# A hybrid DiT layer on one core: where the residual's store stands in the DMA queue, the order of the last chunk of a first group, and who scales the output

## The chip, the cores and the metric

One NeuronCore of a Trainium2 chip runs the whole layer. The metric is device time in microseconds (us), the median of several executions. TensorE (PE) multiplies, VectorE (DVE), ScalarE (ACT) and GpSimd (POOL) work on elements, SyncE (SP) issues most DMAs. Each engine runs its own instructions in the order in which the program lists them and waits on semaphores, and so does SP: a DMA whose wait is not met holds back every DMA behind it.

## The reference

The input is 1024 latent tokens of width 1024 and 256 context tokens. The layer is a half-step SwiGLU FFN (width 2816), then two token mixers from one input projection (`w_in`, softmax attention and a gated linear attention), merged and projected, then a second half-step FFN and a final RMSNorm.

```python
def half_ffn(h, mod, i, g, w_up, w_down):
    shift, scale, gate = mod[..., 3 * i, :], mod[..., 3 * i + 1, :], mod[..., 3 * i + 2, :]
    return h + 0.5 * gate * swiglu(modulate(rms_norm(h, g), shift, scale), w_up, w_down)
...
        h = half_ffn(h, m_lat, 0, g_norm[l, 0], w_ffn_up[l, 0], w_ffn_down[l, 0])
        hc = half_ffn(hc, m_ctx, 0, g_norm[l, 0], w_ffn_up[l, 0], w_ffn_down[l, 0])
        n_lat = modulate(rms_norm(h, g_norm[l, 1]), m_lat[..., 3, :], m_lat[..., 4, :])
        p_lat = jnp.split(n_lat @ w_in[l], IN_SPLITS, axis=-1)
...
        h = h + m_lat[..., 5, :] * merge_branches(p_lat, attn_lat, gla_lat, g_gla[l], w_branch[l], b_gate[l], w_out[l])
        h = half_ffn(h, m_lat, 2, g_norm[l, 2], w_ffn_up[l, 1], w_ffn_down[l, 1])
    return rms_norm(h, g_final)
```

## The kernel before

**Layout.** Activations stand feature-major in SBUF: 8 tiles k of 128 features by tokens. Tokens come in chunks: 512, 512 and 256 (the context) in the first FFN (`ffn0`) and the input projection (`win`), 512 and 512 in the second FFN (`ffn1`). Every product is made of three float32r matmuls (`three`, L203 to L207), since both operands are split in a high and a low part: `nh`, `nl` (or `n1h`, `n1l`) for the normalized activations, `wh`, `wl` for the weights.

**Weight panels.** Weights arrive as panels of 128 x 1024 in `raw`, which has two slots. VectorE splits a panel into `wh` and `wl` (`split_panel`, L178), which also have two slots each. So the load of panel p waits until panel p-2 is split, and the split of panel p waits until TensorE is done with panel p-2 (`panel_used`). All loads go through SP's queue in program order.

**An FFN group.** `Ffn.pe` goes over 11 groups: four up panels (a, b, a, b; 8 tiles k for each chunk), SiLU on ScalarE, the product and its split on VectorE (`hidden`), and two down panels, whose results VectorE adds to `h`. In the first group of an FFN the normalization is still being made: panels 0 and 1 of a chunk are taken in pairs of tiles by `PAIR_STEPS` (`up_pair`), with a wait for tile k before each (`normed`), except for the last chunk. There TensorE waits once for the last tile, then takes panel 0 for all k, then panel 1. `win_pe` does the same for the first two panels of `w_in` (c == 2 is the last chunk).

**The norm between.** `Norm` squares on ScalarE, sums with matmuls (`sums`, L465), takes the root on ScalarE, the inverse on VectorE, and spreads it over partitions with matmuls into a PSUM bank (`spread`, L487). Then for each tile k: VectorE scales (L499), ScalarE rounds to the high part (L508), VectorE takes the low part (L516). For `ffn1`'s second chunk, `spread` is issued inside the pair steps of the first chunk (`norm2_rest_pe`, at step 11).

**The residual's store.** After `ffn0` the latent `h0` (4 MB) is saved to DRAM, since its SBUF space is needed. In `win_sp` this store stands behind the load of the first `w_in` panel and waits for the last add of `ffn0` (`wait_end`). ScalarE waits for it (`h_saved`) before it writes the first projection results over `h0`.

**The output.** In `ffn1`'s last group the down product goes chunk by chunk in 16 tiles q (six matmuls each). When chunk 0 is done (q up to 7), its four blocks of 128 tokens are turned by TensorE (`y_turn`) into two PSUM banks each, between the tiles of chunk 1; ScalarE squares and takes the root (`y_act`), VectorE takes the reciprocal and multiplies by it and by `g_final` (`y_scale`), SP stores 512 KB (`result_sp`). Then the four blocks of chunk 1. Blocks 2 and 3 use the banks of blocks 0 and 1.

Of the kernel before, what the change touches and what calls it, by code (L numbers as in the profile page):

```python
# [100 lines left out]
def build(nc, x, c, ctx_in, c_ctx, w_mod, b_mod, g_norm, w_ffn_up, w_ffn_down, w_in, g_q, g_k,  # L101
# [8 lines left out]
    def sem(name):  # L110
# [29 lines left out]
    y_ss, y_root, y_inv = at("y_ss", 181, [SEQ // P]), at("y_root", 181.125, [SEQ // P]), at("y_inv", 181.25, [SEQ // P])  # L140
    y_junk = at("y_junk", 174, [D])
    g_row = at("g_row", 201, [D])
    y_rows = at("y_rows", 72, [SEQ // P, D])
    h1 = at("h1", 40, [KT, SEQ])
    n1h, n1l = at("n1h", 0, [KT, SEQ], F32R), at("n1l", 72, [KT, SEQ], F32R)
# [28 lines left out]
    y_turned, y_squared, y_rooted, y_inverse, y_done = (  # L174
        sem(n) for n in ("y_turned", "y_squared", "y_rooted", "y_inverse", "y_done"))


    def split_panel(dve, p, n=1024):  # L178
# [17 lines left out]
    def wait_panel(pe, p):  # L196
# [2 lines left out]

    PAIR_STEPS = [(0, 0), (0, 1), (0, 2), (0, 3), (1, 0), (1, 1), (1, 2), (1, 3),  # L200
                  (0, 4), (1, 4), (0, 5), (1, 5), (0, 6), (1, 6), (0, 7), (1, 7)]

    def three(pe, o, hi_w, lo_w, hi_x, lo_x, first, last):  # L203

# [329 lines left out]
    class Ffn:  # L534
# [44 lines left out]
        def pe(self, pe, in_first, in_last):  # L579
# [22 lines left out]
            def up_pair(g, c):  # L602

                o = [up_bank(g, 0, c), up_bank(g, 1, c)]
                for n, (j, k) in enumerate(PAIR_STEPS):
                    self.norm.normed(pe, c, k)
                    mm = up_k(o[j], j, c, k)
                    if k == KT - 1:
                        mm.then_inc(self.up_done, 1)
                    in_first(c, n)  # L610

            def down(j, n, c, o):
# [7 lines left out]
            def body(g, first, last):  # L620
                if first:
                    wait_panel(pe, self.panel(g, 0))
                    wait_panel(pe, self.panel(g, 1))
                    for c in range(C - 1):
                        up_pair(g, c)
                    self.norm.normed(pe, C - 1, KT - 1)
                    for j in range(2):
                        up(g, j, C - 1)
                for j in range(2 if first else 0, 4):
                    wait_panel(pe, self.panel(g, j))  # L630
                    for c in range(C):
                        up(g, j, c)
                if last:
                    for q in range(8 * C):
                        c, j, n = q // 8, 4 + q % 8 // 4, q % 4
                        if n == 0 and c == 0:
                            wait_panel(pe, self.panel(g, j))
                        if q % 8 == 0:
                            pe.wait_ge(self.hid_done, g * (4 * C) + 2 * (C + c) + 2)
                        if q == 2:  # L640
                            pe.wait_ge(self.hid_done, (g + 1) * (4 * C))
                        pe.wait_ge(self.down_free, self.n_down + g * (8 * C) + max(0, q - 2))
                        mm = down(j, n, c, ps[self.TAIL_BANKS[q % 3]][:, 0:self.chunks[c][1]])
                        mm.then_inc(panel_used if n == 3 and c == C - 1 else self.down_done, 1)
                        in_last(q)
                    return
                for j in range(4, 6):
                    wait_panel(pe, self.panel(g, j))
                    for n in range(4):
                        for c, (t0, w) in enumerate(self.chunks):  # L650
                            i = ((j - 4) * 4 + n) * C + c
                            if j == 4 and n == 0:
                                pe.wait_ge(self.hid_done, g * (4 * C) + 2 * (C + c) + 2)
                            pe.wait_ge(self.down_free, g * (8 * C) + (i + 1))
                            mm = down(j, n, c, ps[self.down_banks[i % self.n_down]][:, 0:w])
                            mm.then_inc(self.down_done if not (n == 3 and c == C - 1) else panel_used, 1)
# [108 lines left out]
    def y_turn(pe, i):  # L765

        ffn1.wait_residual(pe, 7 if i < 4 else 15)
        if i in (2, 3):
            pe.wait_ge(y_done, i - 1)
        if i in (6, 7):  # L770
            pe.wait_ge(y_done, i - 3)
# [11 lines left out]
    def y_scale(dve, i):  # L783
        dve.wait_ge(y_rooted, i + 1)
        nc.vector.reciprocal(y_inv[:, i:i + 1], y_root[:, i:i + 1]).then_inc(y_inverse, 1)
        if i == 0:
            dve.wait_ge(g_row_loaded, 16)
        dve.wait_ge(y_inverse, i + 1)
        nc.vector.scalar_tensor_tensor(y_rows[:, i, :], y_psum(i), y_inv[:, i:i + 1], g_row[:, :], ALU.mult, ALU.mult)\
            .then_inc(y_done, 1)  # L790

    def result_pe(pe, q):

        if q >= 9 and q % 2 == 1:
            y_turn(pe, (q - 9) // 2)
        if q == 15:
            for i in range(4, 8):
                y_turn(pe, i)

    def result_act(act):  # L800
        for i in range(SEQ // P):
            y_act(act, i)

    def result_dve(dve):
        for q in range(16):
            ffn1.last_residual(dve, q)
            if q in (12, 14):
                y_scale(dve, (q - 12) // 2)
        for i in range(2, SEQ // P):
            y_scale(dve, i)  # L810

    def result_sp(sp):
        for i in range(SEQ // P):
            sp.wait_ge(y_done, i + 1)
# [82 lines left out]
    def win_sp(sp, panel0, ffn0, norm):  # L897
        w = w_in[0].rearrange("(k p) n -> p k n", p=P)
        for i, (col, width, _, _) in enumerate(win):
            p = panel0 + i  # L900
            load_panel(sp, pn(p), raw[:, p % 2, 0:KT * width].rearrange("p (k n) -> p k n", k=KT),
                       w[:, :, col:col + width])
            if i == 0:
                ffn0.wait_end(sp)
                sp.dma_start(h_dram, h0[:, :, 0:SEQ]).then_inc(h_saved, 16)

# [49 lines left out]
    def win_pe(pe, panel0, norm):  # L956
# [14 lines left out]
        wait_panel(pe, pn(panel0))  # L971
        ffn0.wait_residual(pe, 22)
        for c in range(3):
            if c == 2:
                norm.normed(pe, c, KT - 1)
                for j in range(2):
                    for k in range(KT):
                        mm = unit_k(2 * c + j, k)
                    done(2 * c + j, mm)
                continue  # L980
            if c == 1:
                ffn0.wait_residual(pe, 23)
            for n, (j, k) in enumerate(PAIR_STEPS):
                if (c, j, k) == (0, 1, 0):
                    wait_panel(pe, pn(panel0 + 1))
                norm.normed(pe, c, k)
# [1016 lines left out]
    @block.gpsimd  # L2003
    def _(pool):
        att_pool(pool)

    @block.vector
    def _(dve):
# [61 lines left out]
```

## Time and profile before

| | us |
|---|---|
| time, median of 3 runs | 3090.2 (3086.2 to 3090.93) |
| the profiled execution's own time | 3087.16 |
| its span, first to last instruction | 3085.1 |
| busy: PE, DVE, ACT, POOL | 2882.0, 1499.4, 552.3, 59.5 |
| mean granted TensorE clock, share of full speed | 0.957 |

A row of a timeline is: start, duration, engine, line, operation, output<-inputs, shape, count, and in brackets the time that the engine sat idle before it with what ended the idle time. Matmuls overlap: with 512 columns each shows 0.39 us and the next one starts earlier than it ends.

### The profile page before, as it was taken

What the parts mean: (1) busy time and instruction counts of PE and PEld (TensorE: products, weight loads), DVE (VectorE), ACT (ScalarE), POOL (GpSimd) and SP (SyncE); (2) the same over time, 40 slices, a digit from 0 to 9 for tenths busy, and PEclk for the clock granted to TensorE, in tenths of its full rate; (3) what the DMA queues carried; (4) which work ended last, traced back from release to release, by engine and by line L of the source; (5) the groups of instructions that cost most, each with busy time, mean ns of one, the idle gap of its engine ahead of it and who ended that gap; (6) DMA issues with size and microseconds to landing.
All of it is one profiled execution on the core that took longest, in us unless ns stands there. A gap on an engine that the chain in (4) does not pass through costs nothing. (4 is left out here: it accounts for less than half of the span.)

```text
span 3085.1 us, 35899 instructions
## 1 busy us (share of the span) xinstructions
PE 2882.0 (93%) x14410; PEld 2298.4 (75%) x14410; DVE 1499.4 (49%) x2403; ACT 552.3 (18%) x1035; POOL 59.5 (2%) x100
## 2 busy tenths in 40 slices
PE   8999999999999799999956859998998999999998
PEld 2588888888888587888245637776877888888887
DVE  5544444444444611111596378886644444444444
ACT  3200000000000311111422247774011000000001
POOL 0000000000000000000000001121000000000000
PEclk9999999999999899999876569999999999999999
DMA  8511111111111211233400100002430111111111
GB/s 289 161 35 41 41 34 41 34 41 34 41 40 36 76 37 48 82 99 103 140 1 1 41 0 1 1 1 69 142 97 27 48 49 48 48 48 41 47 55 69
DMA packets 190653, 176.15 MB, mean 57 GB/s; under 512 B 5805, under 2 KB 147290, under 8 KB 190554
## 3 DMA queue, kind: packets, MB, share of 16 engines
q1 hardware_dynamic: 184794, 164.29, 17.2%
q10 hardware_dynamic: 5760, 10.49, 0.9%
q8 instruction: 69, 1.13, 0.2%
q14 instruction: 30, 0.25, 0.0%
HBM read 155.89 MB, written 18.87 MB: 57 GB/s over the span
## 5 line engine op out<-in xcount | busy, mean ns | idle before, releaser
L205 PE MATMUL psum<-nh,wh 128*128 128x512 f32 (+2 forms) x1688 | 613.6, 364 | 16.0 <-DVE wl L185 15.4
L206 PE MATMUL psum<-nl,wh 128*128 128x512 f32 (+2 forms) x1688 | 613.1, 363 | 0.0
L207 PE MATMUL psum<-nh,wl 128*128 128x512 f32 (+2 forms) x1688 | 612.7, 363 | 0.0
L183 DVE CAST wh<-raw 128x1024 fp32r<-128x1024 f32 x175 | 120.2, 687 | 727.3 <-PE psum L207 699.7
L205 PEld LDWEIGHTS psum<-nh,wh 128*128 128x128 f32 (+1 forms) x1688 | 317.3, 188 | 68.1 <-DVE wl L185 15.5
L206 PEld LDWEIGHTS psum<-nl,wh 128*128 128x128 f32 (+1 forms) x1688 | 317.3, 188 | 50.7
L207 PEld LDWEIGHTS psum<-nh,wl 128*128 128x128 f32 (+1 forms) x1688 | 317.0, 188 | 51.1
L716 DVE SCALAR_TENSOR_TENSOR h<-psum,gates,h 128x512 f32<-128x512 f32 (+1 forms) x400 | 270.9, 695 | 143.6 <-PE psum L207 140.6
L205 PE MATMUL psum<-hidh,wh 128*128 128x512 f32 (+1 forms) x880 | 328.2, 373 | 8.0 <-DVE hidl L700 7.6
L684 ACT ACTIVATE silu_a<-psum 128x512 f32<-128x512 f32 (+1 forms) x110 | 61.2, 556 | 1495.2 <-PE psum L207 1495.2
L206 PE MATMUL psum<-hidl,wh 128*128 128x512 f32 (+1 forms) x880 | 324.9, 369 | 0.0
L207 PE MATMUL psum<-hidh,wl 128*128 128x512 f32 (+1 forms) x880 | 324.0, 368 | 0.0
L205 PE MATMUL psum<-n1h,wh 128*128 128x512 f32 x704 | 275.2, 391 | 8.5 <-DVE n1l L516 8.5
L207 PE MATMUL psum<-n1h,wl 128*128 128x512 f32 x704 | 274.7, 390 | 0.0
L206 PE MATMUL psum<-n1l,wh 128*128 128x512 f32 x704 | 274.7, 390 | 0.0
L695 DVE TENSOR_TENSOR prod<-silu_a,psum 128x512 f32<-128x512 f32 (+1 forms) x110 | 69.9, 635 | 344.9 <-PE psum L207 343.7
L185 DVE TENSOR_TENSOR wl<-raw,wh 128x1024 fp32r<-128x1024 f32 x175 | 213.7, 1221 | 6.0
L205 PEld LDWEIGHTS psum<-hidh,wh 128*128 128x128 f32 x880 | 165.9, 188 | 43.6 <-issue 13.7
L207 PEld LDWEIGHTS psum<-hidh,wl 128*128 128x128 f32 x880 | 165.6, 188 | 28.5
L206 PEld LDWEIGHTS psum<-hidl,wh 128*128 128x128 f32 x880 | 166.0, 189 | 26.7
L205 PEld LDWEIGHTS psum<-n1h,wh 128*128 128x128 f32 x704 | 132.7, 188 | 36.7 <-DVE n1l L516 8.9
L207 PEld LDWEIGHTS psum<-n1h,wl 128*128 128x128 f32 x704 | 132.6, 188 | 27.6
(239 smaller groups left out, 3382.9 us busy)
## 6 DMA issues: line engine op xcount, KB each, us to landing
raw<-in_w_ffn_up_dram SPq DMA_DIRECT2D x88, 512.0 KB, 3.8
mod_raw<-in_w_mod_dram SPq DMA_DIRECT2D x24, 1024.0 KB, 5.1
raw<-in_w_ffn_down_dram SPq DMA_DIRECT2D x44, 512.0 KB, 3.8
raw<-in_w_in_dram SPq DMA_DIRECT2D x34, 512.0 KB, 3.8
mod_raw_late<-in_w_mod_dram SPq DMA_DIRECT2D x12, 1024.0 KB, 5.1
gates_saved<-staged ACTq DMA_DIRECT2D x40, 256.0 KB, 2.0
merge_gate<-gates_saved SPq DMA_DIRECT2D x8, 1024.0 KB, 5.1
x_rows<-in_x_dram SPq DMA_DIRECT2D x8, 512.0 KB, 7.4
```

What stands on the lines that cost most here:

```text
L183: nc.vector.tensor_copy(wh[:, par, 0:n], raw[:, par, 0:n]).then_inc(panel_split, 1)
L185: nc.vector.tensor_tensor(wl[:, par, 0:n], raw[:, par, 0:n], wh[:, par, 0:n].bitcast(F32), ALU.subtract).then_inc(panel_split, 1)
L205: pe.matmul(o, hi_w, hi_x, start=first, stop=False)
L206: pe.matmul(o, hi_w, lo_x, start=False, stop=False)
L207: return pe.matmul(o, lo_w, hi_x, start=False, stop=last)
L684: nc.scalar.activation(silu_a[:, c, 0:w], ps[c][:, 0:w], ACT.Silu).then_inc(self.a_free, 1)
L695: nc.vector.tensor_tensor(prod[:, c % 2, 0:w], silu_a[:, c, 0:w], ps[3 + c][:, 0:w], ALU.mult).then_inc(self.b_free, 1)
L716: nc.vector.scalar_tensor_tensor(hk, down, gates[:, self.gate_i, k, s:s + 1], hk, ALU.mult, ALU.add).then_inc(self.down_free, 1)
```

## The change

Four edits. The store of `h0` stands behind the third panel load of `win_sp` and no longer behind the first. The last chunk of `ffn0`'s, `ffn1`'s and `win`'s first two panels is taken tile by tile in a new order, `LAST_PAIR_STEPS`, with a wait for each tile. `spread` of `ffn1`'s second chunk is issued at pair step 8 and no longer at step 11. The output of chunk 0 is scaled by ScalarE from PSUM into a new buffer (`y_copy`), and multiplied by `g_final` on GpSimd (`y_gain`); the turns of these blocks come one tile q earlier, and they wait for the copy out of PSUM only. VectorE keeps their reciprocals, and the whole of chunk 1.

```diff
+    LAST_PAIR_STEPS = [(0, 0), (0, 1), (0, 2), (0, 3), (1, 0), (0, 4), (1, 1), (0, 5),
+                       (1, 2), (0, 6), (1, 3), (0, 7), (1, 4), (1, 5), (1, 6), (1, 7)]
...
-                for n, (j, k) in enumerate(PAIR_STEPS):
+                for n, (j, k) in enumerate(PAIR_STEPS if c < C - 1 else LAST_PAIR_STEPS):
                     self.norm.normed(pe, c, k)
                     mm = up_k(o[j], j, c, k)
                     if k == KT - 1:
-                        mm.then_inc(self.up_done, 1)
+                        mm.then_inc(self.up_done if c < C - 1 else panel_used, 1)
...
-                    for c in range(C - 1):
+                    for c in range(C):
                         up_pair(g, c)
-                    self.norm.normed(pe, C - 1, KT - 1)
-                    for j in range(2):
-                        up(g, j, C - 1)
...
         if i in (2, 3):
-            pe.wait_ge(y_done, i - 1)
+            pe.wait_ge(y_copied, i - 1)
...
+    def y_copy(act, i):
+        act.wait_ge(y_inverse, i + 1)
+        nc.scalar.activation(y_scaled[:, i, :], y_psum(i), ACT.Copy, scale=y_inv[:, i:i + 1]).then_inc(y_copied, 1)
+
+    def y_gain(pool, i):
         if i == 0:
+            pool.wait_ge(g_row_loaded, 16)
+        pool.wait_ge(y_copied, i + 1)
+        nc.gpsimd.tensor_tensor(y_rows[:, i, :], y_scaled[:, i, :], g_row[:, :], ALU.mult).then_inc(y_gained, 1)
...
     def result_pe(pe, q):
 
-        if q >= 9 and q % 2 == 1:
-            y_turn(pe, (q - 9) // 2)
+        if q >= 8 and q % 2 == 0:
+            y_turn(pe, (q - 8) // 2)
...
             load_panel(sp, pn(p), raw[:, p % 2, 0:KT * width].rearrange("p (k n) -> p k n", k=KT),
                        w[:, :, col:col + width])
-            if i == 0:
+            if i == 2:
                 ffn0.wait_end(sp)
                 sp.dma_start(h_dram, h0[:, :, 0:SEQ]).then_inc(h_saved, 16)
...
-            for n, (j, k) in enumerate(PAIR_STEPS):
+            for n, (j, k) in enumerate(PAIR_STEPS if c < 2 else LAST_PAIR_STEPS):
...
-        if (c, n) == (0, 11):
+        if (c, n) == (0, 8):
             norm2.spread(pe, 1)
```

SP's queue at the end of `ffn0` before the change: the last panels of the FFN, one panel of `w_in`, the store, and the other panels.

```order
L194 DMA raw<-in_w_ffn_up_dram 128x8x128 x4
L194 DMA raw<-in_w_ffn_down_dram 128x2x512 x2
L194 DMA raw<-in_w_in_dram 128x8x128
L905 DMA h_saved<-h_49 1024x1x1024
L194 DMA raw<-in_w_in_dram 128x8x128 x7
```

The same place in the changed kernel:

```order
L195 DMA raw<-in_w_ffn_up_dram 128x8x128 x4
L195 DMA raw<-in_w_ffn_down_dram 128x2x512 x2
L195 DMA raw<-in_w_in_dram 128x8x128 x3
L929 DMA h_saved<-h_49 1024x1x1024
L195 DMA raw<-in_w_in_dram 128x8x128 x5
```

The loads of panels 1 and 2 of `w_in` now stand ahead of the store; panel 3 is the first behind it.

ScalarE's last instructions before the change, for the first three output blocks (a square with its sum, and a root, for each):

```order
L778 ACTIVATE y_junk,y_ss<-psum 128x1024
L780 ACT_TABLE_LOAD
L780 ACTIVATE y_root<-y_ss,cols_b 128x1
L778 ACTIVATE y_junk,y_ss<-psum 128x1024
L780 ACTIVATE y_root<-y_ss,cols_b 128x1
L778 ACTIVATE y_junk,y_ss<-psum 128x1024
```

And in the changed kernel:

```order
L779 ACTIVATE y_junk,y_ss<-psum 128x1024
L781 ACT_TABLE_LOAD
L781 ACTIVATE y_root<-y_ss,cols_b 128x1
L790 ACTIVATE y_scaled<-psum,y_inv 128x1024
L779 ACTIVATE y_junk,y_ss<-psum 128x1024
L781 ACTIVATE y_root<-y_ss,cols_b 128x1
L790 ACTIVATE y_scaled<-psum,y_inv 128x1024
```

A copy of 128x1024 has been put in after each of the first four roots; it needs VectorE's reciprocal, so the next square stands behind that too.

VectorE at the same place before the change (L749 adds a down tile to `h`, L785 is the reciprocal, L789 the product with `g_row`):

```order
L749 SCALAR_TENSOR_TENSOR h_89<-psum,gates,h_89 128x512 x13
L785 RECIPROCAL y_inv<-y_root 128x1
L789 SCALAR_TENSOR_TENSOR y_rows<-psum,y_inv,g_row 128x1024
L749 SCALAR_TENSOR_TENSOR h_89<-psum,gates,h_89 128x512 x2
L785 RECIPROCAL y_inv<-y_root 128x1
L789 SCALAR_TENSOR_TENSOR y_rows<-psum,y_inv,g_row 128x1024
L749 SCALAR_TENSOR_TENSOR h_89<-psum,gates,h_89 128x512
```

And in the changed kernel:

```order
L750 SCALAR_TENSOR_TENSOR h_90<-psum,gates,h_90 128x512 x11
L786 RECIPROCAL y_inv<-y_root 128x1
L750 SCALAR_TENSOR_TENSOR h_90<-psum,gates,h_90 128x512 x2
L786 RECIPROCAL y_inv<-y_root 128x1
L750 SCALAR_TENSOR_TENSOR h_90<-psum,gates,h_90 128x512 x2
L786 RECIPROCAL y_inv<-y_root 128x1
L750 SCALAR_TENSOR_TENSOR h_90<-psum,gates,h_90 128x512
```

Between the adds only reciprocals are left; the four products of chunk 0 are gone from VectorE.

## Rows read from the trace of the kernel before

**Rows 1.** The page, part 1: busy us, share of the span, instructions

```profile
PE 2882.0 (93%) x14410; PEld 2298.4 (75%) x14410; DVE 1499.4 (49%) x2403; ACT 552.3 (18%) x1035; POOL 59.5 (2%) x100
```

**Rows 2.** Waits of TensorE, whole span: us in total, times, longest

```profile
PE psum L205 <- DVE wl L185: 22.3, 3, 15.4
...
PE psum L205 <- DVE n1l L516: 8.5, 1, 8.5
```

**Rows 3.** Timeline of SP's queue, 984 to 1100 us

```profile
987.99 0.37 SPq L194 DMA_DIRECT2D raw<-in_w_in_dram  x1
1042.22 0.63 SPq L905 DMA_DIRECT2D h_saved<-h  x1
1042.89 47.75 SPq L194 DMA_DIRECT2D raw<-in_w_in_dram  x5
```

**Rows 4.** Timeline of VectorE, 1000 to 1100 us, the panels' splits

```profile
1001.56 1.23 DVE L185 TENSOR_TENSOR wl<-raw,wh 128x1024 fp32r<-128x1024 f32 x1
...
1038.46 1.23 DVE L185 TENSOR_TENSOR wl<-raw,wh 128x1024 fp32r<-128x1024 f32 x1
...
1057.96 0.69 DVE L183 CAST wh<-raw 128x1024 fp32r<-128x1024 f32 x1 [15.77 <-DMA raw<-in_w_in_dram]
1058.69 1.23 DVE L185 TENSOR_TENSOR wl<-raw,wh 128x1024 fp32r<-128x1024 f32 x1
...
1085.41 0.69 DVE L183 CAST wh<-raw 128x1024 fp32r<-128x1024 f32 x1 [3.31 <-PE psum L207]
```

**Rows 5.** Timeline of TensorE, 1020 to 1120 us

```profile
1044.16 0.43 PE L465 MATMUL psum<-sq,cst 128*32 128x64 f32 x16
1059.97 0.79 PE L205 MATMUL psum<-nh,wh 128*128 128x512 f32 x1 [15.38 <-DVE wl L185]
...
1088.02 0.40 PE L205 MATMUL psum<-nh,wh 128*128 128x512 f32 x1
```

**Rows 6.** DMA issues: count, KB each, median us to landing

```profile
h_saved<-h SPq DMA_DIRECT2D x1, 4096.0 KB, 13.3
...
out_dram<-y_rows SPq DMA_DIRECT2D x8, 512.0 KB, 2.7
```

**Rows 7.** Windows: length, busy of each engine, PEclk, DMA share, GB/s

```profile
1060.00:1064.00 4.00, 4.00 (x10) 3.13 (x11) 4.00 (x7) 1.64 (x3) 0.00 (x0) 0.50 0.50 131
...
200.00:1040.00 840.00, 839.56 (x4495) 715.97 (x4494) 364.43 (x548) 48.91 (x89) 0.00 (x0) 1.00 0.12 36
```

**Rows 8.** Timeline of VectorE, 2300 to 2385 us

```profile
2337.22 0.75 DVE L516 SCALAR_TENSOR_TENSOR n1l<-scaled_t,modv,n1h 128x512 fp32r<-128x512 f32 x1
...
2345.15 1.62 DVE L516 SCALAR_TENSOR_TENSOR n1l<-scaled_t,modv,n1h 128x512 fp32r<-128x512 f32 x2
...
2349.18 0.69 DVE L700 TENSOR_TENSOR hidl<-prod,hidh 128x512 fp32r<-128x512 f32 x1
```

**Rows 9.** Timeline of TensorE, 2332 to 2362 us

```profile
2334.59 1.05 PE L487 MATMUL psum<-inv_t,cst 128*128 128x128 f32 x8
...
2337.99 0.39 PE L207 MATMUL psum<-n1h,wl 128*128 128x512 f32 x1
2346.83 0.80 PE L205 MATMUL psum<-n1h,wh 128*128 128x512 f32 x1 [8.45 <-DVE n1l L516]
...
2359.54 0.39 PE L207 MATMUL psum<-n1h,wl 128*128 128x512 f32 x1
2359.76 0.39 PE L205 MATMUL psum<-n1h,wh 128*128 128x512 f32 x1
```

**Rows 10.** Timeline of TensorE in the tail: the first turn

```profile
3059.18 1.03 PE L773 MATMUL psum<-cst,h 128*128 128x128 f32 x8
```

**Rows 11.** Timeline of VectorE in the tail: the last product

```profile
3080.73 1.28 DVE L789 SCALAR_TENSOR_TENSOR y_rows<-psum,y_inv,g_row 128x1024 f32<-128x1024 f32 x1
```

**Rows 12.** Groups of ScalarE by shape: the squares (busy us, mean ns, idle)

```profile
L778 ACT ACTIVATE y_junk<-psum 128x1024 f32<-128x1024 f32 x8 | 8.1, 1016 | 33.1 <-PE psum L773 33.1
```

**Rows 13.** Groups of GpSimd: a product of two tensors

```profile
L1770 POOL TENSOR_TENSOR att_t<-att_t,att_rb 64x256 f32<-64x256 f32 x32 | 23.2, 725 | 2069.8 <-DVE att_t L1744 2069.8
```

More of the change, by code:

```diff
@@ L142, in build @@
     g_row = at("g_row", 201, [D])
+    y_scaled = at("y_scaled", 0, [4, D])
     y_rows = at("y_rows", 72, [SEQ // P, D])
@@ L173, in build @@
     g_row_loaded = sem("g_row_loaded")
-    y_turned, y_squared, y_rooted, y_inverse, y_done = (
-        sem(n) for n in ("y_turned", "y_squared", "y_rooted", "y_inverse", "y_done"))
+    y_turned, y_squared, y_rooted, y_inverse, y_copied, y_gained, y_done = (
+        sem(n) for n in ("y_turned", "y_squared", "y_rooted", "y_inverse", "y_copied", "y_gained", "y_done"))
     def split_panel(dve, p, n=1024):
@@ L768, in y_turn @@
         if i in (2, 3):
-            pe.wait_ge(y_done, i - 1)
+            pe.wait_ge(y_copied, i - 1)
         if i in (6, 7):
-            pe.wait_ge(y_done, i - 3)
+            pe.wait_ge(y_copied, i - 3)
         for k in range(KT):
@@ L781, in y_act, with y_reciprocal, y_scale @@
             .then_inc(y_rooted, 1)
-    def y_scale(dve, i):
+    def y_reciprocal(dve, i):
         dve.wait_ge(y_rooted, i + 1)
         nc.vector.reciprocal(y_inv[:, i:i + 1], y_root[:, i:i + 1]).then_inc(y_inverse, 1)
+    def y_copy(act, i):
+        act.wait_ge(y_inverse, i + 1)
+        nc.scalar.activation(y_scaled[:, i, :], y_psum(i), ACT.Copy, scale=y_inv[:, i:i + 1]).then_inc(y_copied, 1)
+    def y_gain(pool, i):
         if i == 0:
+            pool.wait_ge(g_row_loaded, 16)
+        pool.wait_ge(y_copied, i + 1)
+        nc.gpsimd.tensor_tensor(y_rows[:, i, :], y_scaled[:, i, :], g_row[:, :], ALU.mult).then_inc(y_gained, 1)
+    def y_scale(dve, i):
+        if i == 4:
             dve.wait_ge(g_row_loaded, 16)
+        y_reciprocal(dve, i)
         dve.wait_ge(y_inverse, i + 1)
@@ L802, in result_act @@
             y_act(act, i)
+            if i < 4:
+                y_copy(act, i)
     def result_dve(dve):
@@ L806, in result_dve, with result_pool @@
             ffn1.last_residual(dve, q)
-            if q in (12, 14):
-                y_scale(dve, (q - 12) // 2)
-        for i in range(2, SEQ // P):
+            if q >= 10 and q % 2 == 0:
+                y_reciprocal(dve, (q - 10) // 2)
+        y_reciprocal(dve, 3)
+        for i in range(4, SEQ // P):
             y_scale(dve, i)
+    def result_pool(pool):
+        for i in range(4):
+            y_gain(pool, i)
     def result_sp(sp):
         for i in range(SEQ // P):
-            sp.wait_ge(y_done, i + 1)
+            if i < 4:
+                sp.wait_ge(y_gained, i + 1)
+            else:
+                sp.wait_ge(y_done, i - 3)
             sp.dma_start(out[0, i * P:(i + 1) * P, :], y_rows[:, i, :]).then_inc(out_stored[i % 2], 16)
@@ L973, in win_pe @@
         for c in range(3):
[L974 to L980, printed above, removed]
             if c == 1:
                 ffn0.wait_residual(pe, 23)
-            for n, (j, k) in enumerate(PAIR_STEPS):
+            for n, (j, k) in enumerate(PAIR_STEPS if c < 2 else LAST_PAIR_STEPS):
                 if (c, j, k) == (0, 1, 0):
@@ L2005, in _ @@
         att_pool(pool)
+        result_pool(pool)
     @block.vector
```

## The prediction

> **What bounds the kernel now.** I read the busy shares first: TensorE is busy for 2882 of 3085 us [rows 1], so most of the change's places lie on its path, and what it can win there is TensorE's idle time and the clock that it loses by idling. The waits of TensorE [rows 2] give the idle time. Two single waits matter: 15.4 us for the low half of a weight panel (`wl`), and 8.5 us for the last tile of a normalization (`n1l`). Then I read the timelines around both.
>
> The first wait is the change from `ffn0` to `win`. SP loads panel 0 of `w_in` at 987.99 and then stands in the wait of the store until 1042.22; panel 1's load goes out behind the store at 1042.89 [rows 3]. The store takes 13.3 us to land [rows 6] and the panel lands behind it: VectorE has sat idle for 15.77 us when its cast starts at 1057.96, and TensorE goes on at 1059.97, 15.38 us late [rows 4, 5]. The second is the first group of `ffn1`: TensorE is through with chunk 0 at 2338.2 and waits until tile 7 of chunk 1 is ready, 2346.8 [rows 8, 9].
>
> **The store behind panel 2's load.** Panel 1's load then waits for one thing only, the split of the panel two before it, which ends at 1001.56 + 1.23 = 1002.8 [rows 4]; at 15 us or less it has landed long before it is wanted. Panel 2's load waits for the split of panel 0 and goes out at 1038.46 + 1.23 = 1039.7, still ahead of the last add of `ffn0`, so the store leaves at 1042.2 as before. VectorE starts panel 1's split where its idle time began, 1057.96 - 15.77 = 1042.2, and ends at 1044.1; TensorE is done with its 16 small sums at about 1044.55 [rows 5] and goes on at once. That is the whole 15.4 us. What is late next? Panel 3's load: it waits for panel 1's split (1044.1) and lands behind the store at about 1059; it is wanted by its split at about 1070, 11 us of cover. ScalarE's wait for the store: that lands at 1042.2 + 13.3 = 1055.5, and ScalarE is busy with the norm's high parts for another 10 us. VectorE's tiles: its whole chain moves forward by 15.8 us with TensorE, so none is late that was not.
>
> **The clock.** After the pause the granted clock was 0.50 for the 4 us from 1060 to 1064 [rows 7], the lower level of 1.2 GHz; half of these 4 us is lost work, 2.0 us. With no pause ahead of it I take that back too.
>
> **The last chunk tile by tile, in `win`.** TensorE waited only a few tenths there, which I leave in the noise. But the new order has a price. Panel 2 can be split only when panel 0 is used up, and a split takes 0.69 + 0.04 + 1.23 = 1.96 us. Before, the cast began at 1085.41, when eight tiles of panel 1 were left, and TensorE needed panel 2 at 1088.02: 2.61 us, enough. 24 matmuls of 256 columns are 2.9 us, so one is 0.12. Now four tiles are left when panel 0 is done, 12 matmuls or 1.44 us less: 2.61 - 1.44 = 1.17 us for 1.96 us of work, a new wait of 0.8 us. `win` together: 15.4 + 2.0 - 0.8 = **16.6 us**.
>
> **`ffn0`.** The same order, the same 256 columns, and no wait for tiles to remove, since that norm is finished long before. So only the price: **-0.8 us**.
>
> **`ffn1`.** Two edits. `spread` comes three steps earlier; a step is three matmuls at 0.227 us (2359.54 to 2359.76 is one pitch), so 2.05 us: it moves from 2334.59 to 2332.5, and VectorE's chain on chunk 1 with it. The low parts end at 2337.97 (tile 0) and from there one in 1.32 us (2337.22 to 2345.15 is six tiles), the last at 2346.77 [rows 8]. Shifted: 2335.9, 2337.2, 2338.6, 2339.9, 2341.2, 2342.5, 2343.8, 2344.7. TensorE begins chunk 1 at 2338.2 and takes one step per 0.68 us; by the new order it wants tile 3 at 2340.3, tile 4 at 2341.6, tile 5 at 2343.0, tile 6 at 2344.4, tile 7 at 2345.7. Every one is there 0.4 us or more ahead. So chunk 1 ends at 2338.2 + 48 x 0.227 = 2349.1, where it ended at 2359.76 [rows 9]. Here too panel 2 is next. VectorE first finishes `hidden` of chunk 0, at 2349.18 + 0.69 - 2.05 = 2347.8 (ScalarE's SiLU stands behind the high parts, which moved by the same), then splits: 2349.75. TensorE waits 0.6 us. 2359.76 - 2349.75 = **10.0 us**, of which 8.5 are the wait and the rest mostly the slow matmuls after it. Without the earlier `spread`, tiles come 2.05 us later and TensorE would lose 1.7 us to them.
>
> **The tail.** The first turn was at 3059.18 [rows 10]; it moves up by one tile (1.36 us) to 3057.8. From there seven tiles q and four turns of 0.8 us follow, none of which waits if ScalarE's copies come in time. A copy of 128x1024 out of PSUM is priced by the square of the same shape, 1.02 us [rows 12], and the chain square, root, reciprocal, copy gives copies done at about 3063.5, 3067.2, 3070.8 and 3073.5; the turns that need the first two come at 3065.0 and 3068.7. The last add of chunk 1 ends at about 3071.8. ScalarE reaches block 4's root at 3075.0, and VectorE's four products at 1.39 each end at 3080.6, where the last one ended at 3082.0 [rows 11]: 1.4 us. GpSimd's product is not in the trace at this size. Its product of 64x256 takes 0.725 us [rows 13]; four times the columns is at most 2.9 us, and VectorE's own product, 1.28, is the bound below. I take 2.9: the four end at 3066.4, 3070.1, 3073.7 and 3076.6. Then five stores of 512 KB leave from 3076.6 on. That stores land faster than one per 1.39 us the trace doesn't show; at that pace the last lands at 3076.7 + 4 x 1.39 + 2.7 = 3085.0 against 3084.8 before [rows 6]. So the tail is worth -0.2 to 1.4 us; I take the middle, **0.6**. In a sentence of its own: the Trainium skill ("GPSIMD Engine Reference", section 3.1) advises against elementwise products on GpSimd, at 4497 ns for 2048 columns against 2293 on VectorE; half of that, 2.25 us as an estimate, would let the last product end 0.65 us sooner than mine does, so the rule's price does no harm where the work is off the path.
>
> **Sum.** 16.6 - 0.8 + 10.0 + 0.6 = 26.4 us. The profiled execution took 3087.16 us, so it would be 3060.8. That execution is 3.0 us below the median of the three runs; from the median it is 3063.8. I put the forecast between, at 3062. A change under 0.2% (6 us) is about what a measurement can't tell from none.
>
> **The rivals.**
> 1. *One of the two big waits comes back in part (3070, chance 0.08).* In `ffn1` the tiles lead TensorE by only 0.4 us, and a wait that then starts would be repaid tile by tile; in `win` panel 3 may be late behind the store. Against it: a lead of 0.4 us costs at most what the chain is late in all (1.7 us by the sum above), and 11 us of cover. Half of the 10 us and 3 of `win` lost give 3070.
> 2. *The tail loses (3073, 0.03).* SP stores in order, so blocks 4 to 7 stand behind GpSimd's last product. If that product took twice my bound, 5.8 us, the four would end from 3069.3 to 3086.7, and five stores at 1.39 us would land at 3095.0, 10.2 us after the present end: 3062 + 0.6 + 10.2 = 3073. Against it: four times the row of 0.725 us is all that the width can cost if time goes with columns. Up to 2.9 us the tail loses nothing to speak of; from about 3.7 us on each product waits for the one before, and each further 1 us costs 4.
> 3. *The store's move doesn't do it (3077, 0.04).* If panel 1 were held by something else, or ScalarE's wait for the store stood on the path, 15 us stay. The queue's rows speak against it: the issue came 0.04 us after the store's.
> 4. *Slower (3100, 0.02).* The pauses are the only rests of TensorE in its dense stages; without them the chip might grant less clock. TensorE is dense for some 1880 us, so the gain is gone at 26.4 / 1880 = 1.4% less clock, and 3100 needs 1.9%. Against it: 840 us at 99.9% busy were granted 1.00 throughout, and the only low clock nearby came after a pause [rows 7].
>
> **How the numbers follow.** My forecast has 0.81. The runs before spread over 4.7 us, which the range must hold: from 3086.2 - 26.4 - 2 for tail and new waits, 3057.5, to rival 1's edge, 3069. That leaves out rivals 2, 3 and 4, and part of 1. All cases but rival 4 are over 0.2% faster; a small chance goes to no change, 0.02.
>
> **What would show it.** Right: no idle time of VectorE for `in_w_in`; TensorE's waits for `wl` at three places of 0.6 to 0.9 us; the wait for `n1l` gone, with no clock of 0.50 near either place; GpSimd's product between 2.2 and 2.9 us; last product on VectorE about 1.4 us nearer to the last turn's start. Wrong: a wait for `raw` on panel 3, waits for `n1l` or `nl` in pieces, stores queued behind GpSimd, or another granted clock in the attention stages, where it stood between 0.5 and 1 and where a shift of 16 us may fall out either way.

## The result, and the profile after

The changed kernel takes 3060.28 us in the median of 4 runs (3057.38 to 3064.43); the kernel before took 3088.38 on the same chip (3086.2 to 3090.93). The ratio is 0.991, with a 95% interval of 0.9893 to 0.9927: 28.1 us less. The forecast was 3062, the range 3057.5 to 3069. The profiled execution took 3064.43 us, the slowest of its four; its span is 3062.6 us and its mean clock 0.959, where the one of before had 3085.1 and 0.957.

The busy times of the page of the changed kernel, as in [rows 1]:

```profile
PE 2882.0 (94%) x14410; PEld 2300.6 (75%) x14410; DVE 1494.6 (49%) x2399; ACT 556.8 (18%) x1039; POOL 69.0 (2%) x104
```

TensorE's busy time and count are the same to the last digit, but that is chance, since it moved in every part. Windows over `win`'s first panels (stretch B below), before and after, with the columns of [rows 7]:

```profile
1042.20:1093.70 51.50, 36.12 (x190) 30.14 (x190) 27.32 (x45) 14.72 (x28) 0.00 (x0) 0.83 0.41 133
...
1044.40:1079.20 34.80, 34.12 (x190) 28.85 (x189) 27.12 (x45) 14.70 (x27) 0.00 (x0) 1.00 0.51 173
```

The same 190 matmuls take 2.00 us less of busy time, since none of them runs at the granted clock of 0.50 any more, and from stretch D on it is 2.27 less (731.05 for 733.32). Ahead of the store it is 2.16 more (1031.10 for 1028.94) and in stretch C 2.15 more (1085.75 for 1083.60), where the instructions are the same but for the order of one chunk; the last section takes up C. TensorE's waits for `wl`, as in [rows 2], and no row for `n1l` any more:

```profile
PE psum L209 <- DVE wl L186: 9.0, 5, 6.3
```

The longest, 6.3 us, was one of the three of before too (22.3 in all less 15.4 leaves 6.9 for two). SP's queue, as in [rows 3]:

```profile
990.17 52.10 SPq L195 DMA_DIRECT2D raw<-in_w_in_dram  x3
1044.40 0.63 SPq L929 DMA_DIRECT2D h_saved<-h  x1
1046.26 43.69 SPq L195 DMA_DIRECT2D raw<-in_w_in_dram  x4
```

Three loads now go ahead of the store, and panel 3's goes out 1.9 us behind it, when panel 1 has been split. The timeline of VectorE from 1044 us on, as in [rows 4]:

```profile
1044.29 0.68 DVE L184 CAST wh<-raw 128x1024 fp32r<-128x1024 f32 x1
...
1071.43 0.70 DVE L184 CAST wh<-raw 128x1024 fp32r<-128x1024 f32 x1 [3.00 <-PE psum L211]
1072.16 1.23 DVE L186 TENSOR_TENSOR wl<-raw,wh 128x1024 fp32r<-128x1024 f32 x1
```

The 15.77 us in which VectorE waited for the panel are gone. The cast at 1071.43 is panel 2's, and now it waits for TensorE to use up panel 0. The timeline of TensorE in the same stretch, as in [rows 5]:

```profile
1046.34 0.43 PE L469 MATMUL psum<-sq,cst 128*32 128x64 f32 x16
...
1073.44 0.50 PE L209 MATMUL psum<-nh,wh 128*128 128x512 f32 x1 [0.68 <-DVE wl L186]
```

The same timeline at the same step of `ffn0`, and in `ffn1` as in [rows 9]:

```profile
146.02 0.50 PE L209 MATMUL psum<-nh,wh 128*128 128x512 f32 x1 [0.68 <-DVE wl L186]
...
2337.96 0.50 PE L209 MATMUL psum<-n1h,wh 128*128 128x512 f32 x1 [0.51 <-DVE wl L186]
```

These are the three small waits that the forecast put at 0.8, 0.8 and 0.6 us. The windows of the two places, as in [rows 7]: the clock is at its higher level of 2.4 GHz (1.00) throughout, and TensorE busy for 28.76 of 29.40 us and 12.49 of 13.00 us.

```profile
1044.00:1073.40 29.40, 28.76 (x167) 24.39 (x165) 25.70 (x45) 15.10 (x27) 0.00 (x0) 1.00 0.49 174
2325.00:2338.00 13.00, 12.49 (x56) 10.01 (x55) 11.54 (x18) 6.66 (x9) 0.00 (x0) 1.00 0.00 0
```

**The tail.** Before the change TensorE's turns waited for VectorE's products, which held the PSUM banks: two of the three places on its timeline (the third waited 0.52 us):

```profile
3067.61 1.06 PE L773 MATMUL psum<-cst,h 128*128 128x128 f32 x8 [1.02 <-DVE y_rows L789]
...
3072.40 3.68 PE L773 MATMUL psum<-cst,h 128*128 128x128 f32 x32 [0.97 <-DVE y_rows L789]
```

In the changed kernel no turn waits for a product; the one wait left is for the last add of chunk 1:

```profile
3050.27 3.71 PE L774 MATMUL psum<-cst,h 128*128 128x128 f32 x32 [0.84 <-DVE h L750]
```

On the timeline of ScalarE, the third copy out of PSUM:

```profile
3048.07 1.12 ACT L790 ACTIVATE y_scaled<-psum,y_inv 128x1024 f32<-128x1024 f32 x1 [1.20 <-DVE y_inv L786]
```

On the timeline of GpSimd, the last product:

```profile
3051.94 2.37 POOL L796 TENSOR_TENSOR y_rows<-y_scaled,g_row 128x1024 f32<-128x1024 f32 x1 [0.32 <-ACT y_scaled L790]
```

On the timeline of VectorE, its first product and its last, as in [rows 11]:

```profile
3053.50 1.28 DVE L803 SCALAR_TENSOR_TENSOR y_rows<-psum,y_inv,g_row 128x1024 f32<-128x1024 f32 x1
...
3057.66 1.28 DVE L803 SCALAR_TENSOR_TENSOR y_rows<-psum,y_inv,g_row 128x1024 f32<-128x1024 f32 x1
```

And the DMA issues, as in [rows 6]:

```profile
h_saved<-h SPq DMA_DIRECT2D x1, 4096.0 KB, 13.0
...
out_dram<-y_rows SPq DMA_DIRECT2D x8, 512.0 KB, 2.9
```

GpSimd is through with its fourth product (block 3) at 3054.31, VectorE with its first (block 4) at 3054.78, 0.47 us later, and with its last at 3058.94.

**Where the time came from.** To add the parts up, I cut both traces at the same instructions. The cuts are: VectorE's second product of `ffn0`'s first group (A begins), the issue of the store (B), ScalarE's first gate of `win`'s panel 2 (C), VectorE's last add of the merge (D), ScalarE's SiLU of `ffn1`'s panel 2 (E), the end of VectorE's last product (F, up to the end of the span). B's beginning in the changed kernel is the store above. VectorE's rows for the beginnings of A and D:

```profile
139.64 0.69 DVE L696 TENSOR_TENSOR prod<-silu_a,psum 128x512 f32<-128x512 f32 x1 [9.00 <-PE psum L211]
...
2313.65 0.75 DVE L1947 SCALAR_TENSOR_TENSOR h<-psum,gates,h 128x512 f32<-128x512 f32 x1 [4.62 <-PE psum L211]
```

ScalarE's rows for those of C and E:

```profile
1079.22 0.60 ACT L1035 ACTIVATE gk_f<-psum 128x512 f32<-128x512 f32 x1 [6.03 <-PE psum L211]
...
2343.73 0.60 ACT L685 ACTIVATE silu_a<-psum 128x512 f32<-128x512 f32 x1 [8.37 <-PE psum L211]
```

So B, for one, is 1079.22 - 1044.40 = 34.82 us. The same differences for every kernel of this study, each from its one profiled execution:

| kernel | A `ffn0` | B `win` | C | D `ffn1` | E | F stores |
|---|---|---|---|---|---|---|
| before | 903.79 | 51.47 | 1231.77 | 39.94 | 716.61 | 3.09 |
| after | 904.76 | 34.82 | 1234.43 | 30.08 | 715.21 | 3.66 |
| c0 after again | 904.73 | 34.83 | 1233.98 | 30.08 | 715.20 | 3.67 |
| c1 store only | 903.81 | 35.60 | 1233.50 | 39.96 | 716.58 | 3.18 |
| c2 steps only | 904.76 | 52.34 | 1234.22 | 30.07 | 716.47 | 3.16 |
| c3 tail only | 903.66 | 50.95 | 1231.99 | 39.91 | 715.10 | 3.68 |
| c4 row order | 903.82 | 33.89 | 1232.14 | 30.10 | 715.09 | 3.72 |
| c5 spread at 11 | 904.76 | 34.84 | 1233.63 | 32.16 | 715.23 | 3.70 |
| c6 gain twice | 904.61 | 34.83 | 1234.12 | 30.08 | 715.08 | 10.09 |
| c7 store at 1 | 904.73 | 34.82 | 1234.21 | 30.08 | 715.10 | 3.71 |
| c9 all three | 903.67 | 33.87 | 1234.64 | 29.28 | 715.35 | 3.63 |
| c10 store twice | 904.62 | 34.84 | 1233.62 | 30.08 | 715.20 | 3.67 |
| c11 split first | 904.73 | 34.84 | 1228.57 | 29.28 | 715.20 | 3.70 |
| c12 row and split | 903.79 | 33.88 | 1235.67 | 29.28 | 715.21 | 3.69 |

From before to after: A -0.97, B +16.65, D +9.86, E +1.40, F -0.57. That is 26.4 us. The spans differ by 22.5, since C, whose instructions are the same in both, took 2.66 us more, and the stretch ahead of A 1.21 more. A, B, D, E and F repeat within 0.16 us where nothing in them was changed, but for one thing: the pause in B is not the same from run to run. TensorE's wait after it, in c3 and in c2:

```profile
1060.91 0.80 PE L206 MATMUL psum<-nh,wh 128*128 128x512 f32 x1 [14.89 <-DVE wl L186]
...
1063.13 0.80 PE L209 MATMUL psum<-nh,wh 128*128 128x512 f32 x1 [16.01 <-DVE wl L186]
```

With 15.38 before that is a spread of 1.1 us in three executions, so a gain in B against the one trace of before is known to about half a us, and no better. C does not repeat, and is taken up at the end.

A wait costs more than its number in brackets. A matmul of 512 columns shows 0.39 us, but the next one starts 0.227 us after it, and the first one behind a wait takes 0.34 us to the next start: 0.16 + 0.11 = 0.27 us on top of each bracket.

### The profile page after: what moved, and what is told of

Its sections match the earlier page's. It is cut to its first block and busy times, and to the rows that moved or that the text cites. A ratio compares the mean times of both kernels' runs of the same rounds, so it can differ in the third digit from the quotient of the medians.

```text
span 3062.6 us, 35904 instructions
## 1 busy us (share of the span) xinstructions
PE 2882.0 (94%) x14410; PEld 2300.6 (75%) x14410; DVE 1494.6 (49%) x2399; ACT 556.8 (18%) x1039; POOL 69.0 (2%) x104
```

## The experiments

**c0, c1, c2, c3: the change again, and its three parts alone.** c0 is the changed kernel as it is. c1 is the kernel before with one edit:

```diff
             load_panel(sp, ...)
-            if i == 0:
+            if i == 2:
                 ffn0.wait_end(sp)
```

c2 is the changed kernel with the store back at `i == 0` and the tail of before, so that the new order of steps and the earlier `spread` remain. c3 is the kernel before with the tail of the changed one.

> The changed kernel once more, as the measure for the others. If the split of the gain by places is right (16.8 us in win, 10.0 in ffn1, 0.8 lost in ffn0, 0.8 won in the tail), 26 to 27 us less than before, and the same four numbers in its trace. If the 28 us of the medians are the change's own, and not the spread of runs, the extra 1 to 2 us must turn up at one of these places.

> Only the store's place changed. My theory: the 15.4 us wait goes and so do 2.0 us of half clock after it; but TensorE now reaches the last chunk of win while its tiles are still made, and since it waits once for the last of them it loses about 1.4 us there: 16 us less than before. Rival: the wait was also held by the store's drain through ScalarE, then 5 us or less are won. Rival: the clock falls in win anyway, then 14 us.

> Only the order of the last chunks and the earlier spread. My theory: 10.0 us won in ffn1, 0.8 lost in ffn0, 0.6 lost in win (the store's wait stays there and hides nothing of it): 8.6 us less than before. Rival: in ffn1 the new order only spreads the wait over the tiles, then 3 us or less are won.

> Only the output of chunk 0 on ScalarE and GpSimd. My theory: VectorE's last product ends 1.4 us nearer to the end of ffn1's last group, and the last store lands 0.6 us later after it, so 0.8 us less than before, too little for the medians to tell; the trace of the tail must show it. Rival: ScalarE's longer chain makes the tail 1 us longer or more.

Medians, with the kernel before at 3091.18 us on this chip:

| kernel | us | ratio, 95% | less than before |
|---|---|---|---|
| c0 | 3062.71 | 0.9909 (0.9894 to 0.9924) | 28.5 |
| c1 | 3074.24 | 0.9948 (0.9934 to 0.9961) | 16.9 |
| c2 | 3081.66 | 0.997 (0.996 to 0.9981) | 9.5 |
| c3 | 3089.58 | 0.9998 (0.9988 to 1.0007) | 1.6 |

The parts add up to 28.0 us against 28.5 for the whole, so the medians don't show them to lean on each other; but their intervals are 6 to 9 us wide, and could not. The traces are finer, and show that inside `win` they do. TensorE's one wait in that part of c1:

```profile
1067.66 0.39 PE L205 MATMUL psum<-nh,wh 128*128 128x256 f32 x1 [1.44 <-DVE nl L516]
```

Before, no wait for `nl` stood there: the norm went on while TensorE stood still for the panel. With the pause gone the norm's last tile is late, and c1 wins 15.87 us in B, not the 17.4 of pause and clock. Taking the last chunk with a wait for each tile takes that wait away; with its 0.27 it is worth 1.71 us. In c2, where the pause is still there, the new order wins nothing: B is 0.87 us longer than before. That isn't all its price, since the pause alone was 0.63 us longer in this run; what the trace shows of the order is a new wait for `wl` of 0.68 us. VectorE's cast of panel 1 in c2:

```profile
1061.12 0.69 DVE L184 CAST wh<-raw 128x1024 fp32r<-128x1024 f32 x1 [16.42 <-DMA raw<-in_w_in_dram]
```

c3's tail wins 1.51 us in E and gives back 0.59 in F: 0.9, and its median can't tell that from nothing.

**c4: the last chunk of `ffn0` and `win` row by row.** The waits for each tile stay, but all eight tiles go through panel 0 first, then through panel 1, so eight tiles are left when panel 2 may be split, as before.

```diff
+    ROW_STEPS = [(j, k) for j in range(2) for k in range(KT)]
...
-                for n, (j, k) in enumerate(PAIR_STEPS if c < C - 1 else LAST_PAIR_STEPS):
+                for n, (j, k) in enumerate(PAIR_STEPS if c < C - 1 else ROW_STEPS if self.f == 0 else LAST_PAIR_STEPS):
...
-            for n, (j, k) in enumerate(PAIR_STEPS if c < 2 else LAST_PAIR_STEPS):
+            for n, (j, k) in enumerate(PAIR_STEPS if c < 2 else ROW_STEPS):
```

> The changed kernel, but in ffn0 and win the last chunk is taken panel by panel again, with a wait for each tile (panel 0 for all k, then panel 1). My theory: the two new waits of 0.7 us for wl go, since panel 0 is used up eight tiles before the end, and no wait for tiles comes in their place, since in win VectorE makes one tile in 0.79 us from 1063.0 on and TensorE wants tile 7 at about 1069.4: 1.4 us less than the changed kernel. Rival: the tiles are late in win, and 1 us of wait for nl takes the place of the 0.7.

Measured with c5, c6 and c7 beside 3089.47 for before: 3061.64 us, ratio 0.9912 (0.9897 to 0.9927). In the trace TensorE waits for nothing in B; A is 0.94 and B 0.93 us shorter than in the changed kernel. A is back at what it was before the change. So the price of the new order is the split of panel 2, and the place of that split sets it: a wait of 0.68 us and the 0.27 behind it, 0.95. Against c1, whose order is the same but for the one wait for all tiles, B is 1.71 us shorter: 1.44 + 0.27. B is now 17.58 us under before; pause and clock were put at 17.4, and the pause is uncertain by half a us.

**c5: `spread` at step 11 as before.** What the earlier `spread` is worth, with tiles in the new order:

```diff
-        if (c, n) == (0, 8):
+        if (c, n) == (0, 11):
```

> The changed kernel with the spread of ffn1's second chunk back at step 11. My theory: the tiles come 2.05 us later, TensorE waits for n1l in pieces of 0.3 to 0.7 us, hidden of chunk 0 and the split of panel 2 come 2.05 us later too: ffn1 loses 2.0 us against the changed kernel. Rival: the tiles lead TensorE by enough and nothing changes.

3063.62 us, ratio 0.9917 (0.9903 to 0.993). D is 2.08 us longer. Timeline of TensorE in `ffn1`'s first group:

```profile
2324.33 0.40 PE L211 MATMUL psum<-n1h,wl 128*128 128x512 f32 x1
2325.00 0.50 PE L209 MATMUL psum<-n1h,wh 128*128 128x512 f32 x1 [0.27 <-DVE n1l L520]
2325.34 0.39 PE L210 MATMUL psum<-n1l,wh 128*128 128x512 f32 x1
...
2326.32 0.50 PE L209 MATMUL psum<-n1h,wh 128*128 128x512 f32 x1 [0.36 <-DVE n1l L520]
...
2327.64 0.50 PE L209 MATMUL psum<-n1h,wh 128*128 128x512 f32 x1 [0.36 <-DVE n1l L520]
...
2337.46 0.50 PE L209 MATMUL psum<-n1h,wh 128*128 128x512 f32 x1 [0.67 <-DVE wl L186]
```

The wait for `n1l` comes back in pieces, each the gap between VectorE's pace (a tile in 1.32 us: 2326.32 to 2327.64) and TensorE's. D's growth is the whole 2.05 us by which `spread` is later, though those three pieces and the 0.16 more for `wl` are 1.15 us. Most of the rest stands in the starts: from 2324.33 to 2325.34 two matmuls take 1.01 us where 0.45 is their pace, so the first piece costs 0.56 and not 0.27. The three together cost 1.82 by their starts, with the 0.16 that is 1.98 of the 2.08.

**c6: GpSimd's product twice.** A second product into a buffer that nobody reads, ahead of each of the four, makes GpSimd's work in the tail twice as long:

```diff
+        nc.gpsimd.tensor_tensor(y_twice[:, i, :], y_scaled[:, i, :], g_row[:, :], ALU.mult)
         nc.gpsimd.tensor_tensor(y_rows[:, i, :], y_scaled[:, i, :], g_row[:, :], ALU.mult).then_inc(y_gained, 1)
```

> The changed kernel with each of GpSimd's four products done twice (once into a spare buffer), 4.8 us for a block. My theory: the products chain and the fourth ends at about 19.2 us after the first began, 3061.3 in the changed kernel's time; SP then issues five stores in a row. At the pace of one store in 1.39 us the end comes 7 to 8 us later than in the changed kernel; if stores land faster when they queue, one in 1.0 us, 5.5 to 6 us later. Rival: the DMA queue takes five stores at once, then 2.5 us.

3067.99 us, ratio 0.993 (0.9917 to 0.9944). That is 4.4 us more than c7, whose times are those of the changed kernel (3063.58, below), and F is 6.4 us longer; the 2 us between lie within the spread of the runs. The timeline of GpSimd, its last product:

```profile
3057.55 2.34 POOL L798 TENSOR_TENSOR y_rows<-y_scaled,g_row 128x1024 f32<-128x1024 f32 x1
```

And the window from 3060 to 3065, when only stores were left:

```profile
3060.00:3065.00 5.00, 0.00 (x0) 0.00 (x0) 0.00 (x0) 0.00 (x0) 0.00 (x0) 0.50 0.87 347
```

The product ends at 3059.89, VectorE was done at 3058.11, and all five stores left leave from 3059.91 on, the last at 3062.8, so SP issues them faster than they land. The span ends at 3068.2, 8.3 us later, where one store alone takes 3.09 (F of before): (8.3 - 3.09) / 4 = **1.30 us** for each further store of 512 KB. That is the number that the trace of before did not have. It also gives the end of the changed kernel. There, the store of block 3 leaves at 3054.31 and four follow: 3054.31 + 4 x 1.30 + 3.09 = 3062.60, and the span is 3062.6. By VectorE's last product alone it would be 3058.94 + 3.09 = 3062.03; the 0.57 us between are F's growth. In c6 GpSimd's fourth product ends 1.78 us after VectorE's last, in the changed kernel 4.63 us ahead of it: 6.41 us, and F grew by 6.43. So GpSimd's last product and the queue behind it set the end, and each us that this product took longer would be a us of the whole.

**c7: the store behind panel 1's load, not panel 2's.**

```diff
-            if i == 2:
+            if i == 1:
```

> The changed kernel with the store behind the load of panel 1 of w_in, not panel 2. My theory: panel 2's load then lands behind the store at about 1060, and its split isn't due before 1071, so nothing changes: within 1 us of the changed kernel. Rival: the store delays the next panels past their splits, then a new wait of VectorE for raw and 2 us or more lost.

3063.58 us, ratio 0.9913 (0.9898 to 0.9928); each stretch from A to F is that of c0 within 0.25 us. SP's queue:

```profile
990.67 15.20 SPq L195 DMA_DIRECT2D raw<-in_w_in_dram  x2
1044.88 0.63 SPq L929 DMA_DIRECT2D h_saved<-h  x1
1045.56 44.87 SPq L195 DMA_DIRECT2D raw<-in_w_in_dram  x5
```

Panel 2's load now stands behind the store, lands 14.3 us after its issue, at 1059.9, and still comes in time for its cast at 1071.92. All of the 15.4 us hangs on panel 1's load alone.

**c9, c11, c12: what is left of the small waits.** c11 splits panel 2 of `ffn1` ahead of `hidden` of chunk 0:

```diff
+                if first and self.f == 1:
+                    split_panel(dve, self.panel(g, 2))
+                    hidden(g, 0, range(C))
-                if first:
+                elif first:
                     hidden(g, 0, range(C - 1))
                     split_panel(dve, self.panel(g, 2))
```

c12 is c11 with c4's order. c9 is both, and VectorE's last product and its store in two halves of 512 columns:

```diff
-        nc.vector.scalar_tensor_tensor(y_rows[:, i, :], ...)
+        for cols in ([slice(0, 512), slice(512, D)] if i == 7 else [slice(0, D)]):
+            nc.vector.scalar_tensor_tensor(y_rows[:, i, cols], ...)
```

> The changed kernel, only with VectorE's split of panel 2 ahead of hidden of chunk 0 in ffn1's first group. My theory: the wait of 0.5 us for wl in ffn1 goes, and nothing else moves: 0.5 us, to be seen in the trace alone. Rival: hidden of chunk 0 comes 2 us later and holds up the up panels' banks.

> The changed kernel with three edits: in ffn0 and win the last chunk panel by panel with a wait for each tile; in ffn1's first group VectorE splits panel 2 ahead of hidden of chunk 0; VectorE's last product in two halves of 512 columns, each with a store of its own. My theory: 1.9 us from the first (0.9 in each), 0.5 us from the second, and 0.3 to 0.6 us from the third, since the last store is half as large but the queue is near its pace: 2.8 us less than the changed kernel, 29 to 31 less than before. Rival for the third: two stores cost the second's issue and nothing is won.

> The changed kernel with the last chunk panel by panel in ffn0 and win, and panel 2's split first in ffn1, without the halved last product. By the traces of the single edits: 0.9 us in ffn0, 0.9 in win, 0.8 in ffn1, 2.7 us less than the changed kernel in these segments and no wait of TensorE for wl in any of them; of the medians that is a third of their spread.

c11: 3060.56 us, ratio 0.9911 (0.9894 to 0.9927), and c9: 3060.01, 0.9905 (0.9889 to 0.9922), beside 3090.24 for before; c12: 3058.98, 0.9905 (0.9888 to 0.9921), beside 3087.81. In c11 D is 0.80 us shorter and the wait for `wl` is gone; c12 has A, B and D each as in the single edits, together 2.7 us under the changed kernel. The medians differ by less than their runs spread, so that rests on the traces. The halves won nothing. The timeline of VectorE in c9, its last product:

```profile
3053.76 1.41 DVE L809 SCALAR_TENSOR_TENSOR y_rows<-psum,y_inv,g_row 128x512 f32<-128x512 f32 x2
```

SP's queue, the second half's issue:

```profile
3055.19 0.75 SPq L848 DMA_DIRECT2D out_dram<-y_rows  x1
```

And the DMA issues, the half stores:

```profile
out_dram<-y_rows SPq DMA_DIRECT2D x2, 256.0 KB, 3.1
```

Two halves take 1.41 us for the 1.28 of the whole and the second issue alone 0.75. Above all the end does not hang on the last product, but on the queue from GpSimd's fourth product on (c6), and the queue has the same bytes to store: that product ends at 3050.41, and 3050.41 + 4 x 1.30 + 3.09 = 3058.70, where the span is 3058.8.

**c10: the store twice.** A second store of `h0` into a tensor of its own, right behind the first, and both are waited for. What does a store twice as long do to panel 3, whose cover was put at 11 us?

```diff
+                sp.dma_start(h_dram2, h0[:, :, 0:SEQ]).then_inc(h_saved, 16)
```

> The changed kernel with the 4 MB residual stored twice in a row (to two places; ScalarE and the later load wait for both). It measures the cover. The second store lands at about 25 us after the first's issue, panel 3 of w_in some 4 us behind it, 30 us after the issue. If my 11 us of cover is all there is, the split of panel 3 is late and time is lost, 1 to 2 us. If the cover is larger, since TensorE doesn't want panel 3 before it is through with panel 2, nothing changes, and only VectorE waits for raw.

3061.67 us, ratio 0.9914 (0.9897 to 0.9931), and A to F as in c0 within 0.4 us. SP's queue, the second store:

```profile
1043.57 2.38 SPq L931 DMA_DIRECT2D h_saved<-h  x1
```

The timeline of VectorE, the casts of panels 2 and 3:

```profile
1069.93 0.69 DVE L184 CAST wh<-raw 128x1024 fp32r<-128x1024 f32 x1 [3.02 <-PE psum L211]
...
1071.80 0.69 DVE L184 CAST wh<-raw 128x1024 fp32r<-128x1024 f32 x1
```

The second store landed 22.8 us after its issue, at 1066.4, the first 13.1 after its own. Panel 3 stood behind both: issued at 1045.99, it landed 22.3 us later, at 1068.3, 3.5 us ahead of its cast at 1071.80, which has no idle time in front. With one store it lands 13.5 us after its issue at 1046.26, at 1059.8, and is split at 1073.31. The cover is 13.5 us and not 11, and the second store used up 10 of them. Neither the panel nor ScalarE's wait comes near the path with one store.

## Why the prediction was right, step by step

- **The store's move.** Right: the 15.77 us of VectorE's idle time are gone, c1 has them alone, and c7 shows that one load decides it. The rival that the move does nothing is out.
- **The clock after the pause.** "I take that back too" holds: the clock reads 1.00 from 1044 to 1073, and c4 won 17.58 us in B where 15.4 + 2.0 were put. The 2.0 can be read apart: the same 190 matmuls of B are busy for 36.12 us before and 34.12 after.
- **The new order in `win`.** The total was right (16.65 against 16.6) on one reason that was wrong. "TensorE waited only a few tenths there, which I leave in the noise" was read from a trace in which the pause itself gave the norm time to get ahead. c1 shows the wait that takes its place, 1.44 us, and by c4 against c1 it costs 1.71, which the order wins. The order's price, put at 0.8, was 0.93 by c4, so it wins 0.78 in all where a loss of 0.8 was put. Reckoned apart, the store's move was 1.5 us too high, and the order 1.6 too low. That the two cancel was luck, and no time of the whole kernel could have told.
- **`ffn0`, -0.8.** 0.97 measured (0.94 by c4), with a wait of 0.68 us. The 0.8 left out, in the main, that the first matmul behind a wait is slower to the next start (0.34 us, not 0.227).
- **`ffn1`, 10.0.** 9.86. No wait for `n1l` came back, and the wait for panel 2 was 0.51 us of 0.6. By c11 its whole price is 0.80. What the earlier `spread` is worth was mis-sized: 2.08 us by c5, not 1.7.
- **The tail, 0.6.** 1.40 - 0.57 = 0.83 in the traces, 0.9 in c3. The last product was put 1.4 us sooner and is. The 0.6 was the middle of a range and no reckoning, so that it is near is in part luck: two terms at its lower end were mis-sized. GpSimd's product took 2.37 us and not the 2.9 of four times the small one; the value taken was the bound, and the cost had a fixed part. The stores' pace was bounded at 1.39 and is 1.30. Both count, since GpSimd's last product and the queue behind it set the end (c6): with 2.9 us it would come 0.5 later. ScalarE's copy took 1.12 us where 1.02 was put. The Trainium skill ("GPSIMD Engine Reference", section 3.1) has a figure for an add of 2048 columns; half of it, 2.25 us as an estimate, is within 0.12 us of the trace. That "the rule's price does no harm where the work is off the path" does not hold for the last of the four products, which is on it.
- **The cover of panel 3, 11 us.** It is 13.5 us in the changed kernel. c10 held the load back by 10 us and saw no loss; where the cover ends wasn't tried.
- **Rivals.** *One wait comes back* showed itself only with an edit undone: the pieces of c5 are its mechanism, and D grew by 2.08 us, where 1.7 was given as the most. *The tail loses* needed a dearer product: with twice the work F rose by 6.4 us. *Slower by the clock*: TensorE's mean clock is 0.959 against 0.957, and the places where the pauses went read 1.00. C took 2.66 us more than before, which lies within the 7 us over which it varies; nothing ties it to the change.
- **The sum.** 26.4 put, 26.4 in the traces. The medians say 28.1 (28.5 in c0); the 2 us between are less than one kernel's runs spread over.

## What to carry to other kernels

A wait is read with its neighbours: a pause lets other engines run ahead and hides waits that appear when it goes, so ask of each place behind a pause what would be late without it. A large store that is queued ahead of a load delays that load by most of its own landing time (here the load landed after 15.1 us and not 3.8, behind a store of 13.3), and one load moved past it can be worth all that the queue can give; a second load moved past it added nothing (c7). Where small gains are to be told apart, cut the traces at the same instructions, since a stretch that nobody touched can move by more than the edit is worth. Price a wait by the starts of the matmuls around it and not by its bracket alone. And where stores queue at the end, ask which product's store starts the queue: that one is on the path, whatever engine makes it.

## What the runs showed of the hardware

Stretch C, 1230 us with the same instructions in all fourteen kernels, took from 1228.57 to 1235.67 us. That is 7 us, where A, B, D, E and F repeat within 0.16, but for the pause; the start of A varies too, from 137.38 us to 140.15. The 18 runs of the kernel before that stand beside c0 spread over as much, from 3085.74 us (mean clock 0.958) to 3092.79 (0.954), with no edit at all. C holds the only long stage in which TensorE has work in pieces and the clock stands between its two levels. Windows of the changed kernel over that stage and over the attention behind it:

```profile
1460.00:1840.00 380.00, 269.91 (x1297) 176.60 (x1296) 262.81 (x442) 120.61 (x165) 0.00 (x0) 0.69 0.11 36
1840.00:2110.00 270.00, 243.91 (x1696) 204.63 (x1697) 223.18 (x516) 205.20 (x486) 55.18 (x90) 1.00 0.00 1
```

One and the same part of that stage, 498 matmuls, in c11:

```profile
1547.50:1666.00 118.50, 73.06 (x498) 62.56 (x498) 93.92 (x137) 27.77 (x29) 0.00 (x0) 0.57 0.00 1
```

And in c12:

```profile
1548.00:1669.00 121.00, 74.86 (x498) 64.27 (x498) 94.02 (x137) 27.78 (x29) 0.00 (x0) 0.61 0.00 1
```

The same work took 2.5 us longer in c12, though its mean clock is the higher one. Two windows inside that part show why. In c11:

```profile
1560.00:1600.00 40.00, 20.43 (x178) 18.97 (x180) 39.80 (x55) 10.02 (x10) 0.00 (x0) 0.54 0.00 0
1600.00:1640.00 40.00, 35.74 (x177) 28.50 (x174) 16.21 (x26) 2.79 (x3) 0.00 (x0) 0.59 0.00 1
```

And in c12:

```profile
1560.50:1600.50 40.00, 19.62 (x174) 18.36 (x176) 39.80 (x55) 10.02 (x10) 0.00 (x0) 0.67 0.00 0
1600.50:1640.50 40.00, 36.45 (x159) 28.91 (x159) 13.82 (x22) 0.28 (x1) 0.00 (x0) 0.50 0.00 1
```

In the first window VectorE is busy for 39.80 of 40 us and sets the pace: c12 has the higher clock there (0.67 for 0.54), and it wins nothing, 55 instructions of VectorE in both. In the second TensorE is the busy one, and c12 has the lower clock (0.50 for 0.59): 159 matmuls are started for 177. So the mean clock over a window doesn't give its time; it counts where TensorE sets the pace. Why the clock rises and falls at one place in one run and at another in the next, no run here settles. It was not tied to any edit: c11 and c12 differ only in the order of steps in `ffn0` and `win`, and c4, with that same order, has 1232.14.

The other number that no trace of before had is the pace of stores in one queue: 1.30 us for each further 512 KB, by c6. That is 403 GB/s (524,288 bytes in 1.30 us); the window above reads 347, with the DMA engines busy for 0.87 of it. A store of 512 KB took 2.7 us to land in the median before. The two of 256 KB in c9 took 3.1, but behind other stores; on ScalarE's queue stores of 256 KB took 2.0 us (page of the profile, `gates_saved`), so no run here gives the time of a half store alone in SP's queue.
